# Decoder layer with mixture of experts: three of each token's four expert rows added by DMA, the fourth by VectorE

## The chip, the cores and the metric

The kernel runs on one core of one Trainium2 chip. The metric is the device time of one execution, in microseconds (us); lower is better. A core has TensorE (matrix products), VectorE, ScalarE, GpSimd and SyncE, which run their own instruction streams and meet at semaphores. DMA transfers are issued by SyncE (its queue is "q1 hardware_dynamic" in the profile) and by GpSimd ("q0 software_dynamic"), and both run on the core's 16 DMA engines.

## What is computed

One decoder layer over 512 tokens of width 1024, in float32: an attention and time-mixing half, whose output is added to `x`, and then a feed-forward half in which each token goes to 4 of 32 experts. Only the end of it matters here:

```
h   = rmsnorm(x, ffn_norm_w)
top 4 of 32 experts for each token, gates = softmax(top values)
y_k = gate_k * (act(h @ mlp1_w[e_k] + mlp1_b[e_k]) @ mlp2_w[e_k] + mlp2_b[e_k])
x   = x + y_0 + y_1 + y_2 + y_3
out = rmsnorm(x, final_norm_w)          # x * rsqrt(mean(x*x) + eps) * w
```

## The kernel before

**Tiles.** The 512 tokens are four groups t = 0..3 of 128, one token to a partition; `x` is an on-chip tile of 128 x 4 x 1024. The experts are visited one after the other (b = 0..31), each for the up to 128 tokens that chose it, and the bodies for b = 2..31 are a loop on every engine. The outer rounds exist for experts chosen by more than 128 tokens; with these inputs only round 0 runs.

**The weight stream.** An expert's weights come in 12 pieces of 1 MB. SyncE loads each piece into one of six slots of `raw` (w_pieces, line 1438) after VectorE is done with the piece six before it (`s_lo`). ScalarE splits off the high part (`hi`, line 1547), VectorE the rest (`lo`, line 1672), both in rings of four slots, and TensorE multiplies (lines 1860, 1863, 1881, 1886).

**Expert rows.** ScalarE scales an expert's output by the gate into `ys`, and GpSimd scatters it (line 1499) into `y_dram` in HBM (expert_rows in the profile), which has four rows for each token, one for each k. GpSimd waits until each scatter has landed before it goes on. The table was filled with zeros earlier, so a row that nobody wrote adds nothing. The view `rows_v[t, :, k, :]` is the k-th row of all tokens of group t: 128 rows of 4 KB, with a pitch of 16 KB in HBM.

**The last two experts** (b = 30 and 31) are not scattered. Their outputs stay on chip as high and low parts (`y_hi`, `y_lo`), and TensorE multiplies them with transposed choice matrices (`choose`, line 1971) and with the gated biases (`down_bias`, line 1966) into PSUM, a pair of banks for each group. VectorE makes the two low parts in `y_rest(0, 4)` and `y_rest(1, 0)` (line 1782); ScalarE makes the high parts (lines 1631, 1635). `s_hot` counts the groups that are complete in PSUM.

**The adding transfers.** After its loop GpSimd waits for the last turned rows (`s_tx`), loads the final norm weight, spread over 128 partitions, into `fw` (which is `xg`, the buffer of gathered rows, line 1513), and then issues 16 transfers of 512 KB that add `rows_v[t, :, k, :]` onto `x[:, t, :]` (line 1519), in the order k = 0..3 and, within k, t = 0, 3, 1, 2 (`LAST_ROWS`). Additions onto the same group must not overlap, so for k > 0 it waits until the previous one of that group has landed (`s_row[t]`).

**The close.** For n, t over `LAST_ROWS`, VectorE waits for `s_hot` and for the four additions of group t and sums PSUM and `x` (line 1801). ScalarE squares and sums the row (line 1639) and takes the root (line 1641); `finish(n)` on VectorE takes the reciprocal (line 1792) and multiplies x by it and by `fw` (line 1796); SyncE stores the result (line 1455). `finish(n - 1)` stands behind the sum of group n in VectorE's order, and `finish(3)` is last.

Of the kernel before, what the change touches and what calls it, by code (L numbers as in the profile page):

```python
# [23 lines left out]
ALU = mybir.AluOpType  # L24
# [3 lines left out]
P = 128  # L28
D = 1024
S = 512  # L30
NT = S // P
# [10 lines left out]
EXPERTS = 32  # L42
TURNS = EXPERTS + 1
INDEXED = EXPERTS + 2
SCATTERED = EXPERTS - 2
LAST_ROWS = (0, 3, 1, 2)
# [1306 lines left out]
def place(b, p):  # L1353

    if isinstance(b, int) and b == 0:
        return p - DOWN
    if isinstance(b, int) and b == EXPERTS + 1:
        return STREAM - DOWN + p
    return b * PIECES + (p - 2 * DOWN)


def raw_slot(b, p):

    return place(b if isinstance(b, int) else 1, p) % RAW
# [9 lines left out]
def experts(nc, d, sb, sem, st, g, route, con, ident, psum, bank, out):  # L1374
# [3 lines left out]
    x, stat, o_t, y_dram, down_b, turned = (g[k] for k in ("x", "stat", "o_t", "y_dram", "down_b", "turned"))  # L1378
# [22 lines left out]
    s_tx, s_xh, s_xl = sem("rows_turned"), sem("x_hi"), sem("x_lo")  # L1401
    s_u, s_x, s_sig, s_act = sem("up_clipped"), sem("gate_times_up"), sem("gate_sigmoid"), sem("act_ready")
    s_ta, s_ah, s_al, s_y, s_scat = sem("act_turned"), sem("act_hi"), sem("act_lo"), sem("y_ready"), sem("rows_scattered")
    s_round, s_stored, s_part = sem("round_moved"), sem("rows_stored"), sem("dma_about_to_start")
    s_st, s_selt, s_yl, s_hot = sem("choice_turned"), sem("choice_copied"), sem("last_y_lo"), sem("last_rows_chosen")
    s_blank = sem("gates_blanked")
    s_row = [sem(f"rows_added{t}") for t in range(NT)]
    s_fw, s_add, s_ss, s_sd, s_rs, s_o, s_out = (sem(n) for n in ("final_w_loaded", "sums_ready", "x3_squared", "x3_deviation", "x3_rstd",
                                                                  "out_ready", "out_stored"))
    s_sel31, s_wiped = sem("last_selected"), sem("expert_rows_wiped")  # L1410
# [3 lines left out]
    fw, final = xg, (uu, sg, av, ys)  # L1414
    gate_last = [tab[:, e, 2:3] for e in (EXPERTS - 2, EXPERTS - 1)]
    rows_v = y_dram.rearrange("(t p k) n -> t p k n", p=P, k=4)
    last_banks = {0: 2, 3: 6, 1: 4, 2: 0}

    pairs = psum[:, 0:4, :].rearrange("p b (n two) -> p (b n) two", two=2)
    block = st.enter_context(nc.Block())  # L1420

    def rounds(eng, run, again=None):
        run(0)
        with eng.Fori(1, ROUNDS) as r:
            flag = eng.value_load(flags[0:1, bass.ds(r, 1)])
            with eng.If(flag == 1):
                if again:
                    again(r)
                run(r)

    @block.sync
    def _(sp):
        def load(r, b, p):

            slot = raw_slot(b, p)
            sp.wait_ge(s_lo, r * STREAM + (place(b, p) + 1))
            src = down_rows(d, b - 2, p) if p < DOWN else gate_up_rows(d, b, p - DOWN)
            sp.dma_start(raw[:, slot].rearrange("p r n -> p (r n)"), src).then_inc(s_raw[slot], 16)

        def rest(r):  # L1440

            for p in range(DOWN + RAW, PIECES):
                load(r, 0, p)
            for p in range(DOWN, PIECES):
                load(r, 1, p)
            with sp.Fori(2, EXPERTS) as b:
                for p in range(PIECES):
                    load(r, b, p)
            for b in (EXPERTS, EXPERTS + 1):
                for p in range(DOWN):  # L1450
                    load(r, b, p)

            for n, t in enumerate(LAST_ROWS):
                sp.wait_ge(s_o, r * NT + (n + 1))
                sp.dma_start(out[0, t * P:(t + 1) * P, :], final[t][:]).then_inc(s_out, 16)

        route["sync"](sp)
        rest(0)
        with sp.Fori(1, ROUNDS) as r:
            flag = sp.value_load(flags[0:1, bass.ds(r, 1)])  # L1460
            with sp.If(flag == 1):
                for p in range(DOWN, DOWN + RAW):
                    load(r, 0, p)
                rest(r)
                sp.wait_ge(s_out, (r * NT + NT) * 16)
                sp.sem_inc(s_part, 1)
        sp.wait_ge(s_out, NT * 16)

    @block.gpsimd
    def _(pool):  # L1470
        def zero_rows():
            nc.gpsimd.memset(xg[:], 0.0).then_inc(s_z, 1)

        g["zero_rows"] = zero_rows
        route["gpsimd"](pool)
        pool.wait_ge(s_z, 1)
        pool.sem_inc(s_stored, 1)
        pool.sem_inc(s_blank, 1)

        def gather(r, m):  # L1480
            pool.wait_ge(s_tab, r * INDEXED + (m + 1))
            pool.wait_ge(s_tx, (r * TURNS + m) * 2 + 1)
            pool.sem_inc(s_part, 1)
            nc.gpsimd.tensor_copy(gath_i[:], tab[:, bass.ds(m, 1), 0:1].rearrange("p a c -> p (a c)")).then_inc(s_gi, 1)  # L1484
            pool.wait_ge(s_gi, r * TURNS + (m + 1))
            pool.sem_inc(s_part, 1)
            nc.gpsimd.indirect_dma_start(xg[:], None, g["h2_dram"], bass.IndirectOffsetOnAxis(gath_i[:, 0:1], 0),  # L1487
                                         bounds_check=S - 1, oob_is_err=False).then_inc(s_gath, 16)

        def prepare(r, e):  # L1490
            pool.sem_inc(s_part, 1)
            nc.gpsimd.tensor_copy(this_i[:], tab[:, bass.ds(e, 1), 1:2].rearrange("p a c -> p (a c)"))
            nc.gpsimd.tensor_copy(this_g[:], tab[:, bass.ds(e, 1), 2:3].rearrange("p a c -> p (a c)")).then_inc(s_this, 1)

        def scatter(r, e):
            pool.wait_ge(s_this, r * SCATTERED + (e + 1))
            pool.wait_ge(s_y, r * EXPERTS + (e + 2))
            pool.sem_inc(s_part, 1)
            nc.gpsimd.indirect_dma_start(g["y_dram"], bass.IndirectOffsetOnAxis(this_i[:, 0:1], 0), ys[:], None,  # L1499
                                         bounds_check=4 * S - 1, oob_is_err=False).then_inc(s_scat, 16)  # L1500
            pool.wait_ge(s_scat, (r * SCATTERED + e) * 16 + 16)
            pool.sem_inc(s_stored, 1)

        def run(r):
            for m in range(3):
                gather(r, m)
            with pool.Fori(2, EXPERTS) as b:
                prepare(r, b - 2)
                gather(r, b + 1)
                scatter(r, b - 2)  # L1510
            pool.wait_ge(s_tx, (r * TURNS + EXPERTS) * 2 + 3)
            pool.sem_inc(s_part, 1)
            nc.gpsimd.dma_start(fw[:], d["final_norm_w"].to_broadcast([P, D])).then_inc(s_fw, 16)
            for k in range(4):
                for t in LAST_ROWS:
                    if k:
                        pool.wait_ge(s_row[t], (r * 4 + k) * 16)
                        pool.sem_inc(s_part, 1)
                    nc.gpsimd.dma_start(x[:, t, :], rows_v[t, :, k, :], accum_op=ALU.add).then_inc(s_row[t], 16)

        def again(r):
            pool.wait_ge(s_o, r * NT)
            pool.sem_inc(s_part, 1)
            nc.gpsimd.memset(turned[:].bitcast(F32), 0.0).then_inc(s_blank, 1)
            nc.gpsimd.memset(xg[:], 0.0).then_inc(s_z, 1)
            pool.wait_ge(s_z, r + 1)
            pool.sem_inc(s_part, 1)
            for n in range(4):
                nc.gpsimd.dma_start(y_dram[n * S:(n + 1) * S, :].rearrange("(a p) n -> p a n", p=P),
                                    xg[:].rearrange("p (a n) -> p a n", a=1).to_broadcast([P, S // P, D])).then_inc(s_wiped, 16)  # L1530
            pool.wait_ge(s_wiped, r * 64)
            pool.sem_inc(s_part, 1)

        rounds(pool, run, again)

    @block.scalar
# [113 lines left out]
    def _(dve):  # L1650
# [73 lines left out]
        def run(r):  # L1724
# [55 lines left out]
            def y_rest(n, first):  # L1780
                dve.wait_ge(s_y, r * EXPERTS + (EXPERTS + n))
                nc.vector.scalar_tensor_tensor(y_lo[n], psum[:, first:first + 2, :].rearrange("p b n -> p (b n)"), gate_last[n],
                                               y_hi[n].bitcast(F32), ALU.mult, ALU.subtract).then_inc(s_yl, 1)

            dve.wait_ge(s_used, r * STREAM + (place(b + 1, 0) + 1 + RING))
            y_rest(0, 4)
            y_rest(1, 0)

            def finish(n):
                t = LAST_ROWS[n]  # L1790
# [6 lines left out]

            for n, t in enumerate(LAST_ROWS):
                dve.wait_ge(s_hot, r * NT + (n + 1))
                dve.wait_ge(s_row[t], r * 64 + 64)  # L1800
                nc.vector.tensor_tensor(x[:, t, :], psum[:, last_banks[t]:last_banks[t] + 2, :].rearrange("p b n -> p (b n)"), x[:, t, :],  # L1801
                                        ALU.add).then_inc(s_add, 1)
                if n:
                    finish(n - 1)
            finish(NT - 1)
# [228 lines left out]
```

## Time and profile before

| | |
|---|---|
| three runs | 1722.74, 1724.41, 1724.60 us; median 1724.41 |
| the profiled execution's own time | 1721.57 us |
| its span in the trace | 1719.7 us |
| mean granted TensorE clock | 0.965 of full speed |
| TensorE matmuls busy | 1586.7 us, 92% of the span |
| VectorE, ScalarE, GpSimd busy | 1409.6, 1051.1, 316.3 us |
| HBM read, written | 454.97 MB, 28.31 MB |

The trace is one execution. Its times are counted from the start of the span, so 1719.7 is the end. Busy shares over the whole span are an average over stages with different limits, and what bounds the last 60 us has to be read there. In the DMA view a line of a queue gives packets, megabytes and the time that its packets took as a share of 16 engines over the window; packets overlap a little, so that share can pass 100%. Time to landing runs from the issue of a transfer to its semaphore.

### The profile page before, as it was taken

To read this page: it belongs to the slowest core of one execution; us is meant where nothing else is said; L and a number is where in the kernel's file an instruction comes from. 1 tells how busy PE (TensorE), PEld (TensorE's weight loads), DVE (VectorE), ACT (ScalarE), POOL (GpSimd) and SP (SyncE) were. 2 spreads that over 40 slices of the span, in tenths; PEclk is the share of its full clock that TensorE was granted. 3 is DMA by queue.
4 is the path that set the end of the run, shared out by engine and by line. 5 is a ranking of instruction groups with operands and counts; after the bars stand their busy time and mean duration, and the time that the engine had idled before them with its cause. 6 is when DMAs were issued, how large, how long until landed. Compare 5 with 4: busy or idle time off the path is not lost.

```text
span 1719.7 us, 27994 instructions
## 1 busy us (share of the span) xinstructions
PE 1586.7 (92%) x10297; PEld 1278.6 (74%) x10298; DVE 1409.6 (82%) x1288; ACT 1051.1 (61%) x970; POOL 316.3 (18%) x223
## 2 busy tenths in 40 slices
PE   5888889887687999999999999999999999999994
PEld 5666667666575888888888888888888888888883
DVE  5857667475647899999999999999999999999984
ACT  5434232232335777777777777777777777777772
POOL 6200000000011112222221222112222121311222
PEclk9999999998788999999999999999999999999997
DMA  5610011000629799999999999999999999999999
GB/s 189 245 36 27 26 38 39 26 2 2 212 103 377 280 367 364 368 351 370 360 375 371 351 374 370 366 377 342 366 364 366 357 358 367 359 363 376 353 326 208
DMA packets 100717, 467.39 MB, mean 272 GB/s; under 512 B 12695, under 2 KB 39351, under 8 KB 51376
## 3 DMA queue, kind: packets, MB, share of 16 engines
q1 hardware_dynamic: 86032, 429.79, 65.7%
q0 software_dynamic: 14624, 36.74, 6.9%
q8 instruction: 45, 0.74, 0.2%
q14 instruction: 16, 0.13, 0.0%
HBM read 454.97 MB, written 28.31 MB: 281 GB/s over the span
## 4 chain that ended last, share of the span: by engine, by line
PE 68%; DMA 3%; DVE 2%; ACT 1%; issue 0%; PEld 0%; POOL 0%; ACTq 0%; DVEq 0%; POOLq 0%; PEldq 0%
PE psum L1860 28%; PE psum L1863 13%; PE psum L1881 13%; PE psum L1886 6%; PE psum L1289 3%; DMA x<-expert_rows 2%; PE psum L1852 2%; PE psum L1842 2%; PE psum L1872 1%; PE psum L1832 1%; DVE w_pieces_lo L1672 1%; ACT w_pieces_hi L1547 0%; PE psum L1305 0%; PE psum L1297 0%; DVE x L1801 0%
## 5 line engine op out<-in xcount | busy, mean ns | idle before, releaser
L1672 DVE TENSOR_TENSOR w_pieces_lo<-w_pieces,w_pieces_hi 128x2048 fp32r<-128x2048 f32 x384 | 871.2, 2290 | 92.6 <-ACT w_pieces_hi L1547 92.6
L1547 ACT ACTIVATE w_pieces_hi<-w_pieces 128x2048 fp32r<-128x2048 f32 x384 | 736.8, 1919 | 295.5 <-PE psum L1863 219.1
L1860 PE MATMUL psum<-w_pieces_hi,xh 128*128 128x512 f32 x1024 | 292.5, 408 | 6.1 <-DVE xl L1683 6.1
L1863 PE MATMUL psum<-w_pieces_lo,xh 128*128 128x512 f32 x1024 | 276.5, 392 | 0.0
L1860 PE MATMUL psum<-w_pieces_hi,xl 128*128 128x512 f32 x1024 | 276.4, 392 | 0.0
L1860 PEld LDWEIGHTS psum<-w_pieces_hi,xl 128*128 128x128 f32 x1024 | 192.9, 188 | 43.0
L1863 PEld LDWEIGHTS psum<-w_pieces_lo,xh 128*128 128x128 f32 x1024 | 192.9, 188 | 42.8
L1860 PEld LDWEIGHTS psum<-w_pieces_hi,xh 128*128 128x128 f32 x1024 | 181.7, 190 | 47.8 <-issue 10.9
L1499 POOL DMA_INDIRECT expert_rows<-ys,this_i x30 | 151.9, 5063 | 247.9 <-issue 247.9
L1881 PE MATMUL psum<-w_pieces_hi,ah 128*128 128x512 f32 x512 | 160.9, 395 | 0.0
L1881 PE MATMUL psum<-w_pieces_hi,al 128*128 128x512 f32 x512 | 158.3, 390 | 0.0
L1886 PE MATMUL psum<-w_pieces_lo,ah 128*128 128x512 f32 x512 | 137.0, 390 | 0.0
L1881 PEld LDWEIGHTS psum<-w_pieces_hi,al 128*128 128x128 f32 x512 | 96.2, 188 | 20.2
L1886 PEld LDWEIGHTS psum<-w_pieces_lo,ah 128*128 128x128 f32 x512 | 96.1, 188 | 20.1
L359 ACT ACTIVATE pall<-psum 128x512 f32<-128x512 f32 x26 | 15.5, 594 | 152.9 <-PE psum L781 152.9
L1881 PEld LDWEIGHTS psum<-w_pieces_hi,ah 128*128 128x128 f32 x512 | 93.7, 188 | 18.1 <-DVE al L1689 0.5
L781 PE MATMUL psum<-h_hi_sb,w_hi_sb 128*128 128x512 f32 x208 | 92.6, 445 | 8.8 <-ACT pall L359 8.8
L1487 POOL DMA_INDIRECT xg<-h_rows,gath_i x33 | 81.4, 2468 | 28.7 <-POOL gath_i L1484 27.4
L781 PE MATMUL psum<-h_hi_sb,w_lo_sb 128*128 128x512 f32 x208 | 84.8, 407 | 0.0
L781 PE MATMUL psum<-h_lo_sb,w_hi_sb 128*128 128x512 f32 x208 | 84.7, 407 | 0.0
L1484 POOL CAST gath_i<-index_table 128x1 int32 (+1 forms) x33 | 9.0, 273 | 371.9 <-PE psum L1842 360.6
L1118 POOL DMA_DIRECT2D w_pieces<-in_ffn_norm_w x1 | 0.5, 547 | 383.9 <-POOLq L159 383.9
(366 smaller groups left out, 1973.7 us busy)
## 6 DMA issues: line engine op xcount, KB each, us to landing
w_pieces<-in_mlp_w SPq DMA_DIRECT2D x384, 1024.0 KB, 6.9
w_raw<-in_w_in SPq DMA_DIRECT2D x26, 512.0 KB, 3.9
expert_rows<-o_t POOLq DMA_DIRECT2D x4, 2048.0 KB, 14.7
x<-expert_rows POOLq DMA_DIRECT2D x16, 512.0 KB, 9.5
w_pieces<-in_w_out SPq DMA_DIRECT2D x8, 512.0 KB, 9.2
chunk_work<-in_x SPq DMA_DIRECT2D x4, 512.0 KB, 5.8
x<-in_x SPq DMA_DIRECT2D x4, 512.0 KB, 14.2
h_rows<-w_pieces POOLq DMA_DIRECT2D x4, 512.0 KB, 2.9
```

The costliest lines, as they stand in the source:

```text
L781: last = nc.tensor.matmul(o, w[:, n % 3, k, :], h[:, k, :], start=k == 0 and m == 0, stop=k == KT - 1 and m == 2)
L1289: last = nc.tensor.matmul(bank(2 * t + c), o[:, k, t * P:(t + 1) * P], w[:, k, c * 512:(c + 1) * 512], start=k == 0 and m == 0, stop=k == ...
L1487: nc.gpsimd.indirect_dma_start(xg[:], None, g["h2_dram"], bass.IndirectOffsetOnAxis(gath_i[:, 0:1], 0), bounds_check=S - 1, oob_is_err=Fal ...
L1499: nc.gpsimd.indirect_dma_start(g["y_dram"], bass.IndirectOffsetOnAxis(this_i[:, 0:1], 0), ys[:], None, bounds_check=4 * S - 1, oob_is_err= ...
L1547: nc.scalar.activation(hi[:, p % RING], raw[:, raw_slot(b, p)].rearrange("p r n -> p (r n)"), ACT.Copy).then_inc(s_hi, 1)
L1672: nc.vector.tensor_tensor(lo[:, p % RING], raw[:, raw_slot(b, p)].rearrange("p r n -> p (r n)"), hi[:, p % RING].bitcast(F32), ALU.subtrac ...
L1842: last = nc.tensor.transpose(bank(into, k * P, k * P + P), xg[:, (4 * q + k) * P:(4 * q + k + 1) * P], ident)
L1852: last = nc.tensor.transpose(bank(into, k * P, k * P + P), rows[:, k // 2, k % 2, :], ident)
L1860: nc.tensor.matmul(bank(c), a[:, k, :], hi[:, p % RING, c * 512:(c + 1) * 512], start=False, stop=False)
L1863: last = nc.tensor.matmul(bank(c), xh[:, k, :], lo[:, p % RING, c * 512:(c + 1) * 512], start=False, stop=k == KT - 1)
L1881: nc.tensor.matmul(bank(into + c), a[:, 2 * p + r2, :], hi[:, p % RING, r2 * D + c * 512:r2 * D + (c + 1) * 512], start=p == 0 and r2 == 0 ...
L1886: last = nc.tensor.matmul(bank(into + c), ah[:, 2 * p + r2, :], lo[:, p % RING, r2 * D + c * 512:r2 * D + (c + 1) * 512], start=False, sto ...
```

## The change

For each group t, the rows k = 0, 1, 2 are still added to `x` by DMA, now from the end of GpSimd's loop on, ahead of the wait for the last turned rows and of the norm weight's load, which stand behind the sixth addition. The order of the twelve is written out: (t0,0) (t1,0) (t2,0) (t3,0) (t0,1) (t1,1), the norm weight, (t0,2) (t1,2) (t2,1) (t3,1) (t2,2) (t3,2), where t0..t3 are the groups 0, 3, 1, 2. The row k = 3 is loaded by SyncE, by a plain transfer, into two rows of `o_t`, an on-chip tile that is free by then, after SyncE's last weight load and after all scatters have landed. VectorE adds it to `x` in `add_row(n)`, which waits for the three additions of its group and for the plain load, and counts `s_sum`. `add_row(0)` and `add_row(1)` stand behind `y_rest(0, 4)` and `y_rest(1, 0)`; `add_row(2)` and `add_row(3)` stand behind the sums of the first and the second group.

```diff
+    def row3(t):
+        return o_t[:, 2 * t:2 * t + 2, :].rearrange("p a s -> p (a s)")
@@ SyncE, behind its last weight load
+            sp.wait_ge(s_scat, (r * SCATTERED + SCATTERED) * 16)
+            for t in LAST_ROWS:
+                sp.dma_start(row3(t), rows_v[t, :, 3, :]).then_inc(s_row3[t], 16)
@@ GpSimd, behind its loop over the experts
-            pool.wait_ge(s_tx, (r * TURNS + EXPERTS) * 2 + 3)
-            pool.sem_inc(s_part, 1)
-            nc.gpsimd.dma_start(fw[:], d["final_norm_w"].to_broadcast([P, D])).then_inc(s_fw, 16)
-            for k in range(4):
-                for t in LAST_ROWS:
-                    if k:
-                        pool.wait_ge(s_row[t], (r * 4 + k) * 16)
-                        pool.sem_inc(s_part, 1)
-                    nc.gpsimd.dma_start(x[:, t, :], rows_v[t, :, k, :], accum_op=ALU.add).then_inc(s_row[t], 16)
+            t0, t1, t2, t3 = LAST_ROWS
+            for t, k in ((t0, 0), (t1, 0), (t2, 0), (t3, 0), (t0, 1), (t1, 1), (t0, 2), (t1, 2), (t2, 1), (t3, 1), (t2, 2), (t3, 2)):
+                if k:
+                    pool.wait_ge(s_row[t], (r * 3 + k) * 16)
+                    pool.sem_inc(s_part, 1)
+                nc.gpsimd.dma_start(x[:, t, :], rows_v[t, :, k, :], accum_op=ALU.add).then_inc(s_row[t], 16)
+                if t == t1 and k == 1:
+                    pool.wait_ge(s_tx, (r * TURNS + EXPERTS) * 2 + 3)
+                    pool.sem_inc(s_part, 1)
+                    nc.gpsimd.dma_start(fw[:], d["final_norm_w"].to_broadcast([P, D])).then_inc(s_fw, 16)
@@ VectorE, its close
+            def add_row(n):
+                t = LAST_ROWS[n]
+                dve.wait_ge(s_row[t], r * 48 + 48)
+                dve.wait_ge(s_row3[t], r * 16 + 16)
+                nc.vector.tensor_tensor(x[:, t, :], x[:, t, :], row3(t), ALU.add).then_inc(s_sum, 1)
+
             y_rest(0, 4)
+            add_row(0)
             y_rest(1, 0)
+            add_row(1)
...
             for n, t in enumerate(LAST_ROWS):
                 dve.wait_ge(s_hot, r * NT + (n + 1))
-                dve.wait_ge(s_row[t], r * 64 + 64)
+                dve.wait_ge(s_sum, r * NT + (n + 1))
                 nc.vector.tensor_tensor(x[:, t, :], psum[:, last_banks[t]:last_banks[t] + 2, :].rearrange("p b n -> p (b n)"), x[:, t, :],
                                         ALU.add).then_inc(s_add, 1)
+                if n < 2:
+                    add_row(n + 2)
                 if n:
                     finish(n - 1)
             finish(NT - 1)
```

## Rows read from the trace of the kernel before

**Rows 1.** The page: shares of the chain that ended last, by engine.
```profile
PE 68%; DMA 3%; DVE 2%; ACT 1%; issue 0%; PEld 0%; POOL 0%; ACTq 0%; DVEq 0%; POOLq 0%; PEldq 0%
```

**Rows 2.** That chain in order of time: start us, us, what; the end.
```profile
1663.05 0.58 POOL xg L1513
...
1664.21 10.94 DMA x<-expert_rows
...
1695.99 0.51 issue
1696.50 9.39 DMA x<-expert_rows
1705.98 1.23 DVE x L1801
```

**Rows 3.** Timeline of GpSimd: start us, us, instruction [idle before it, releaser].
```profile
1642.24 5.06 POOL L1499 DMA_INDIRECT expert_rows<-ys,this_i  x1 [8.26 <-issue]
1663.05 0.58 POOL L1513 DMA_DIRECT2D xg<-in_final_norm_w  x1 [15.74 <-PEq L1947]
1663.62 3.61 POOL L1519 DMA_DIRECT2D x<-expert_rows  x4
1673.06 0.85 POOL L1519 DMA_DIRECT2D x<-expert_rows  x1 [5.83 <-DMA x<-expert_rows]
...
1701.48 0.86 POOL L1519 DMA_DIRECT2D x<-expert_rows  x1 [1.48 <-DMA x<-expert_rows]
```

**Rows 4.** DMA view, 1670 to 1706: queue, packets, MB, share.
```profile
q0 software_dynamic: 2063, 7.53, 105.8%
```

**Rows 5.** Timeline of TensorE: the first al, and the last matmuls.
```profile
1692.32 1.52 PE L1971 MATMUL psum<-al,xh 128*128 128x512 f32 x6
...
1695.49 0.61 PE L1971 MATMUL psum<-al,xh 128*128 128x512 f32 x2
```

**Rows 6.** Timelines of VectorE, then SyncE: the close.
```profile
1703.51 1.23 DVE L1801 TENSOR_TENSOR x<-psum,x 128x1024 f32<-128x1024 f32 x1 [13.99 <-DMA x<-expert_rows]
1705.98 1.23 DVE L1801 TENSOR_TENSOR x<-psum,x 128x1024 f32<-128x1024 f32 x1 [1.25 <-DMA x<-expert_rows]
...
1708.58 1.22 DVE L1801 TENSOR_TENSOR x<-psum,x 128x1024 f32<-128x1024 f32 x1
...
1714.07 1.28 DVE L1796 SCALAR_TENSOR_TENSOR av<-x,stat,xg 128x1024 f32<-128x1024 f32 x1
...
1715.38 0.33 SPq L1455 DMA_DIRECT2D out<-av  x1
```

**Rows 7.** DMA view, 4 to 6, plain loads: packets, MB, share.
```profile
q1 hardware_dynamic: 203, 0.77, 95.4%
```

**Rows 8.** The last five scatters (line 1499, 1500 to 1720).
```profile
DMA to landing us min/median/max: 12.4/12.6/13.0
```

**Rows 9.** DMA view, 1666 to 1668.
```profile
q0 software_dynamic: 52, 0.21, 62.6%
q1 hardware_dynamic: 43, 0.24, 29.9%
```

**Rows 10.** DMA view, 1658 to 1666.
```profile
DMA packets 384, 2.82 MB, mean 352 GB/s; under 512 B 40, under 2 KB 40, under 8 KB 40
...
q1 hardware_dynamic: 384, 2.82, 100.4%
```

**Rows 11.** DMA view, 1644 to 1648.
```profile
q1 hardware_dynamic: 216, 1.64, 99.2%
```

**Rows 12.** Timelines of SyncE and ScalarE: last load, last split.
```profile
1661.42 0.33 SPq L1438 DMA_DIRECT2D w_pieces<-in_mlp_w  x1
...
1676.70 1.92 ACT L1547 ACTIVATE w_pieces_hi<-w_pieces 128x2048 fp32r<-128x2048 f32 x1
```

**Rows 13.** DMA view, 1652 to 1654, a scatter beside weights.
```profile
q1 hardware_dynamic: 95, 0.66, 80.8%
q0 software_dynamic: 84, 0.12, 16.4%
```

**Rows 14.** Timeline of VectorE: the second y_rest.
```profile
1688.23 1.28 DVE L1782 SCALAR_TENSOR_TENSOR al<-psum,index_table,ah 128x1024 fp32r<-128x1024 f32 x1 [3.44 <-ACT ah L1635]
```

**Rows 15.** Plain 512 KB stores from GpSimd (line 1130).
```profile
DMA to landing us min/median/max: 2.9/2.9/3.0
```

**Rows 16.** DMA view, 1710 to 1712.
```profile
q0 software_dynamic: 6, 0.01, 3.3%
```

More of the change, by code:

```diff
@@ L1407, in experts @@
     s_row = [sem(f"rows_added{t}") for t in range(NT)]
+    s_row3 = [sem(f"last_row_loaded{t}") for t in range(NT)]
+    s_sum = sem("rows_summed")
     s_fw, s_add, s_ss, s_sd, s_rs, s_o, s_out = (sem(n) for n in ("final_w_loaded", "sums_ready", "x3_squared", "x3_deviation", "x3_rstd",
```

## The prediction

> **What bounds the kernel now.** I read the page first, then the chain of waits over the last 80 us, then the timelines of GpSimd, VectorE, ScalarE, TensorE and SyncE there, and last the DMA view cut into short windows.
>
> Over the whole span TensorE holds 68% of the chain [rows 1]. The change touches none of that; it touches the last 60 us. There the chain runs through one thing: from 1663.05 to 1705.98 it is the expert rows being added to x by DMA, then VectorE's closing work [rows 2]. GpSimd shows the order: the last scatter is issued at 1642.24, the norm weight's load at 1663.05, four additions behind it, then one addition each time an earlier one of the same token group has landed; the last is issued at 1701.48 [rows 3]. Meanwhile the software queue moves 7.53 MB in the 36 us from 1670 with its engines' time full (105.8%) [rows 4]. One addition is 512 KB = 0.524 MB, so 0.524 / (7.53 / 36) = 2.5 us each; 16 cost 40 us. So this stretch is bound by DMA throughput, not latency, and what counts is how much DMA work stands ahead of the closing work. TensorE's last matmuls begin at 1695.49 [rows 5]: it has some 10 us to spare.
>
> How the end hangs on landings: VectorE's second sum (t=3) starts at 1705.98 when the 14th addition lands, and from there sums and final multiplies run back to back until the last output store, 1719.7 - 1705.98 = 13.7 us in all [rows 2, 6]. Additions 15 and 16 land behind that VectorE work at nearly its pace.
>
> **The change part by part.**
>
> *Which landing sets the end.* VectorE's order becomes: sum t=0, row-add t=1; sum t=3, row-add t=2, then finish(0), sum, finish(1), sum, finish(2), finish(3). The row-add of the last group waits for that group's third addition, which is the last transfer of all (T), and everything that followed the second sum before now follows this row-add. A row-add is a 128x1024 tensor-tensor add; the nearest row is the sum from PSUM, 1.22 us [rows 6]. It takes the place of the second sum, of the same length. So end = T + 13.7, where before it was (14th landing) + 13.7: two extra row-adds are early and idle-covered, but finish(0) no longer overlaps the last landings. The row-add for t=1 and sum t=3 (2.5 us) fit just between the last two landings, 2.5 us apart.
>
> *DMA work ahead of T.* Before, 14 additions and the norm weight; after, 12 additions, the norm weight and four plain row loads. The weight's load cancels wherever it stands. Two additions fewer: -5.0 us. Four plain loads: a plain load of 4 KB rows through SyncE's queue moved 0.77 MB in 2 us at 95.4% [rows 7], hence 1.3 us per 0.524 MB, or +5.2 us. This is the cheap bound; the dear one is an addition's 2.5 us (+10.0). I take 1.3: same kind of queue, packet and direction.
>
> *Earlier start.* The last scatter lands 12.6 us after issue [rows 8], at 1654.8; 0.5 us from landing to next issue [rows 2] gives 1655.3 for the first addition instead of 1663.6. The first data lags: the norm weight issued at 1663.05 has no packet in its queue before 1666, and then 62.6% of the 2 us up to 1668 [rows 9], so 3.4 us. Additions thus flow from 1658.7 instead of 1666.5. But the engines are not free then: expert weights move 2.82 MB in 1658 to 1666, 352 GB/s at a share of 100.4% [rows 10], against 1.64 MB in 4 us, 410 GB/s, when the queue is full [rows 11]. Spare is 14% of 7.8 us = 1.1 us, because SyncE's loads are gated by freed slots. Bounds: 0 (the share says full) and, were the traffics independent, all of it (rival below). I take 1.1. Of the 8.3 us gained in issue, only this is worth anything; the rest delays weights.
>
> *The delayed weights.* Sharing halves, the remaining 2.8 MB (6.9 us alone) lasts until 1658.7 + 13.8 = 1672.5, where the last load, issued at 1661.42, had its split at 1676.70 [rows 12]. So nothing is late. At a third of the share it would end at 1679.4, and TensorE would be 2.7 us late, still inside its 10 us. That the two queues do share follows from the scatter, whose 84 packets went beside 95 of weights in 2 us [rows 13].
>
> *Waits on GpSimd and SyncE.* The wait for the turned rows (met at 1663.05) now stands behind the sixth addition; that is issued only after two landings, later than 1663, so it holds up nothing. The row loads stand behind SyncE's last weight load and the scatter wait, met at 1654.8; behind them are only the stores. They take 12.1 us of engine time together with the weights, all spent before 1658.7 + 24.2 = 1683.
>
> *The new wait on VectorE.* Row-add t=0 stands between the two y_rest steps, and waits for the seventh addition. The norm weight with latencies cost 1673.06 - 1666.5 - 2.5 - 0.6 (weights) = 3.5 us [rows 3, 9]; 1658.7 + 7 x 2.5 + 3.5 + 12.1 = 1691.8. The second y_rest, at 1688.23 before [rows 14], then starts at 1693.0 and ends at 1694.3, while TensorE wanted it at 1692.32 [rows 5]. TensorE ends 2 us later, near 1698. VectorE needs the first choice only by 1701, so this is covered; the cover is some 6 us.
>
> *Fewer transfers in flight.* The last two additions wait for those just ahead, with only one other in flight. If landing to next data takes over 2.5 us, engines idle. Beside weights it takes 0.5 + 3.4 = 3.9, a 1.4 us hole; in a quiet queue a 512 KB store landed 2.9 us after issue, data included [rows 15], leaving 1.6 + 0.5 = 2.1 and no hole. Weights are gone by then: I take 0, bounds 0 to 1.4. The Trainium skill, DMA: Bandwidth & Descriptors, Anatomy of one DMA, gives about 2.0 us fixed for a transfer from GpSimd plus bytes over 436 GB/s: by that, an estimate, no hole either, but 1.2 us per row load, so a sum 0.4 us lower than by the row, whose measured rate I use.
>
> **Sum.** T = 1705.98 - 5.0 + 5.2 - 1.1 = 1705.1; end 1718.8 against 1719.7: 0.9 us less. The profiled execution took 1721.57 for its span of 1719.7, so 1720.7; the median is 2.8 above that execution, so 1724.41 - 0.9 = 1723.5. The forecast is no change: a 0.2% step, 3.4 us, is about what a measurement of this kernel can tell from none. Its own bounds: no spare (+1.1), the hole (+1.4), and the last landings: after 1710 the queue moves only 0.01 MB [rows 16], so additions 15 and 16 took 4.2 us from 1705.98, not 5.0. If the last landings come 0.8 us closer together, T is 0.8 earlier, or VectorE, still at its two instructions, eats that again. With all of it, 1722.7 to 1726.0.
>
> **Rivals.** *Additions overlap weights for free (faster).* If additions are limited by their own queue, T = 1658.7 + 12 x 2.5 + 3.5 = 1692.2, and TensorE's end (first choice at 1693.3) leads: three VectorE adds of 1.22 and 13.7 us give 1710.7, a median of 1715.4. For: share read 105.8% at half the bytes. Against: 211 GB/s is half of 410, as if an addition carried its bytes twice through full engines, and nothing of the first addition landed before 1673. Partial overlap gives part of it. Chance 0.15.
>
> *Row loads cost as much as additions (slower).* Each at 2.5: +4.8, so 1728.3. For: short rows at a 16 KB pitch, never loaded so here. Against: [rows 7]. It decides above 2.4 us a load. Chance 0.10.
>
> *Mixing wastes engine time (slower).* In 1666 to 1668, 0.24 MB of weights (0.6 us at 410 GB/s) and 0.21 MB of the software queue (1.0 us at 209) fill 1.6 of 2 us [rows 9]: 20% lost. Over 24.2 mixed us that is 4.8 us, so 1728.3; it passes 0.2% from 18%. Against: that window holds the queue's start. Chance 0.11.
>
> *The change does not do what it says.* The VectorE add replaces a DMA addition, yet the row still travels; if the software queue gets little share while weights run, the early start gains nothing: 1724.6, inside the forecast.
>
> **Chances.** Forecast 0.64, rivals 0.15, 0.10, 0.11. Faster by over 0.2%: 0.16; within: 0.63; slower: 0.21. The range 1720.0 to 1728.6 leaves out most of the free overlap and a little above.
>
> **What the profile would show.** First addition issued near 1655.3; software queue busy beside weights from 1659; row loads landed by about 1684; row-add t=0 near 1692 with y_rest behind it; the last addition landing near 1705; VectorE back to back for 13.7 us from there. A last landing before 1702 would speak for overlap; after 1708, for dear loads or mixing losses, told apart by the megabytes in mixed windows. TensorE's last choice after 1703 would make the new VectorE wait the cause.

## The result, and the profile after

The changed kernel is slower: 1726.57 us median of 20 runs against 1724.40 of 20 runs before, ratio 1.0015 with a 95% interval of 1.0008 to 1.0022, so +2.6 us (0.0015 x 1724.4; the interval reaches from +1.4 to +3.8 us). The forecast was -0.9 us. The size of the step is within the 0.2% that I called no change, but its sign is the other one and clear of the noise.

GpSimd's timeline of the kernel after answers to [rows 3]:

```profile
1643.24 5.07 POOL L1508 DMA_INDIRECT expert_rows<-ys,this_i  x1 [8.26 <-issue]
1656.63 3.68 POOL L1525 DMA_DIRECT2D x<-expert_rows  x4 [8.33 <-DMA expert_rows<-ys,this_i]
1668.44 0.86 POOL L1525 DMA_DIRECT2D x<-expert_rows  x1 [8.13 <-DMA x<-expert_rows]
1673.40 0.86 POOL L1525 DMA_DIRECT2D x<-expert_rows  x1 [4.10 <-DMA x<-expert_rows]
1673.97 0.85 POOL L1529 DMA_DIRECT2D xg<-in_final_norm_w  x1
1685.18 0.85 POOL L1525 DMA_DIRECT2D x<-expert_rows  x1 [10.35 <-DMA x<-expert_rows]
1688.95 2.61 POOL L1525 DMA_DIRECT2D x<-expert_rows  x3 [2.93 <-DMA x<-expert_rows]
1698.71 0.85 POOL L1525 DMA_DIRECT2D x<-expert_rows  x1 [7.15 <-DMA x<-expert_rows]
1701.19 0.85 POOL L1525 DMA_DIRECT2D x<-expert_rows  x1 [1.62 <-DMA x<-expert_rows]
```

The last scatter is issued 1.0 us later than in the trace of before, a difference of these two executions that lies ahead of anything the change touches. To be free of it I count from that issue below. The additions do start 7 us earlier. But look at the end: from 1689 GpSimd issues three at once, then nothing for 7.15 us, then the last two. The order is behind the first gap too. GpSimd issues strictly in the written order, and (t0,2) and (t1,2), which wait for landings at 1684.6 and 1688.4, stand ahead of (t2,1) and (t3,1), whose predecessors had landed at 1677.0 and 1680.8 (semaphore times of this trace). VectorE's timeline answers to [rows 6, 14]:

```profile
1692.44 1.22 DVE L1800 TENSOR_TENSOR x<-x,o_t 128x1024 f32<-128x1024 f32 x1 [6.66 <-DMA x<-expert_rows]
1693.59 1.28 DVE L1792 SCALAR_TENSOR_TENSOR al<-psum,index_table,ah 128x1024 fp32r<-128x1024 f32 x1
...
1705.26 1.23 DVE L1800 TENSOR_TENSOR x<-x,o_t 128x1024 f32<-128x1024 f32 x1 [7.18 <-DMA x<-expert_rows]
1706.40 1.22 DVE L1819 TENSOR_TENSOR x<-psum,x 128x1024 f32<-128x1024 f32 x1
1709.22 1.23 DVE L1800 TENSOR_TENSOR x<-x,o_t 128x1024 f32<-128x1024 f32 x1 [1.59 <-DMA x<-expert_rows]
...
1717.30 1.28 DVE L1814 SCALAR_TENSOR_TENSOR av<-x,stat,xg 128x1024 f32<-128x1024 f32 x1
```

The last landing is at 1709.2, that is 66.0 us after the last scatter's issue, where I had 1705.1 - 1642.2 = 62.9. From there to the end at 1722.9 it is 13.7 us, as forecast. The whole error is in the landing. The DMA view shows where; lines are queue, packets, MB, share, for 1674 to 1684, 1690 to 1698, 1698 to 1702 and 1704 to 1708 in this order:

```profile
q0 software_dynamic: 376, 1.35, 67.5%
q1 hardware_dynamic: 377, 1.41, 37.2%
...
q0 software_dynamic: 417, 1.51, 103.1%
...
q0 software_dynamic: 136, 0.49, 79.2%
...
q0 software_dynamic: 124, 0.44, 58.7%
```

While both queues have work the engines are full (67.5 + 37.2%). Once the additions are alone, they move 1.51 MB in 8 us where [rows 4] gives 1.67, then 0.49 MB in 4 us where it gives 0.84, and 0.44 in 4 near the end. Before, that rate held from 1670 to 1706. In the first of these stretches the engines' time is still full (103.1%) and its packets are longer: 41 of its 369 additions' packets of 4 KB took over 340 ns, where 328 is the rule; in the kernel before it was 11 of 1838 (1670 to 1706). From 1698 on the engines also stand idle (79.2 and 58.7%, the last with the end of the transfers in it). These are holes.

### The profile page after: what moved, and what is told of

Its sections match the earlier page's. It is cut to its first block, busy times and chain, and to the rows that moved or that the text cites. A ratio compares the mean times of both kernels' runs of the same rounds, so it can differ in the third digit from the quotient of the medians.

```text
span 1722.9 us, 27998 instructions
## 1 busy us (share of the span) xinstructions
PE 1585.8 (92%) x10297; PEld 1277.5 (74%) x10298; DVE 1412.4 (82%) x1292; ACT 1051.4 (61%) x970; POOL 313.0 (18%) x219
## 4 chain that ended last, share of the span: by engine, by line
PE 67%; DMA 4%; DVE 2%; issue 1%; ACT 1%; POOL 0%; POOLq 0%; ACTq 0%; DVEq 0%
PE psum L1880 27%; PE psum L1883 13%; PE psum L1901 13%; PE psum L1906 6%; DMA x<-expert_rows 3%; PE psum L1289 3%; PE psum L1872 2%; PE psum L1862 2%; PE psum L1892 1%; DMA expert_rows<-ys,this_i 1%; PE psum L1852 1%; DVE w_pieces_lo L1682 1%; ACT w_pieces_hi L1557 0%; DMA w_pieces<-in_w_out 0%; PE psum L1305 0%
```

## The experiments

Ratios are to the kernel before, timed beside each, with 95% intervals. Four series were timed at different times: the changed kernel; e1 to e4; e6 to e9; changed_again and e10 to e12. changed_again is the changed kernel once more. "Landing" is the last one that VectorE's closing chain waits for; it and "end" are in us, counted from the issue of the last scatter, and come from one trace of each kernel.

| kernel | ratio [95%] | landing | end |
|---|---|---|---|
| before | 1 | 63.7 (14th) | 77.5 |
| changed | 1.0015 [1.0008, 1.0022] | 66.0 | 79.7 |
| changed_again | 1.0013 [1.0004, 1.0022] | 65.1 | 78.9 |
| e1_order | 0.9994 [0.9985, 1.0003] | 62.2 | 75.9 |
| e2_early_only | 0.9996 [0.9987, 1.0005] | 63.1 (14th) | 76.8 |
| e3_rows_only | 1.0008 [0.9998, 1.0018] | 63.3 | 77.1 |
| e4_close | 1.0001 [0.9992, 1.0010] | 68.1 | 78.1 |
| e6_yrest_first | 1.0023 [1.0014, 1.0033] | 65.7 | 79.5 |
| e7_no_row_loads | 0.9996 [0.9987, 1.0006] | 60.4 | 74.1 |
| e8_lone_last | 1.0034 [1.0024, 1.0044] | 69.2 | 83.0 |
| e9_presum | 0.9966 [0.9954, 0.9979] | 62.5 | 71.3 |
| e10_three | 0.9988 [0.9979, 0.9997] | 62.4 | 76.1 |
| e11_presum_uneven | 0.9982 [0.9973, 0.9991] | 67.0 | 75.8 |
| e12_presum_late | 0.9981 [0.9972, 0.9990] | 62.3 | 71.1 |

### e1_order: another order of the additions

```diff
-            for t, k in ((t0, 0), (t1, 0), (t2, 0), (t3, 0), (t0, 1), (t1, 1), (t0, 2), (t1, 2), (t2, 1), (t3, 1), (t2, 2), (t3, 2)):
+            for t, k in ((t0, 0), (t1, 0), (t2, 0), (t3, 0), (t0, 1), (t1, 1), (t2, 1), (t3, 1), (t0, 2), (t1, 2), (t2, 2), (t3, 2)):
```

> The changed kernel with one edit: the twelve additions go row by row (all four groups' k = 0, then k = 1, then k = 2), so that each waits for one issued four places earlier; the norm weight stays behind the sixth. Theory 'holes' (the last additions each had one other transfer in flight, and the time from a landing to the next data let the DMA engines run dry): the last landing comes 3 us earlier than in the changed kernel (1709.2), near 1706, and the kernel is 2 to 3.5 us faster than the changed one, so about equal to the kernel before (-1 to +0.5 us). Rival 'shared engines' (row loads or mixing cost more than the sum): same megabytes, no change, +2.6 us over before. Rival 'VectorE's new wait': row-add t=0 now waits for the ninth addition, some 5 us later, y_rest and TensorE's choices move as far, and the kernel gets slower still, +4 us or more over before.

Measured 0.9994, 0.21% or 3.6 us under the changed kernel's ratio (another series), and -1.0 us against before. The landing moves from 66.0 to 62.2. GpSimd's timeline of e1_order:

```profile
1689.03 0.85 POOL L1525 DMA_DIRECT2D x<-expert_rows  x1 [2.91 <-DMA x<-expert_rows]
1692.90 0.85 POOL L1525 DMA_DIRECT2D x<-expert_rows  x1 [3.02 <-DMA x<-expert_rows]
1695.59 0.85 POOL L1525 DMA_DIRECT2D x<-expert_rows  x1 [1.84 <-DMA x<-expert_rows]
```

and its DMA view, 1690 to 1702:

```profile
q0 software_dynamic: 691, 2.51, 105.8%
```

That is the rate of [rows 4] (209 GB/s) again, without a hole, and only 3 of 613 packets of 4 KB took over 340 ns. "Holes" holds, "shared engines" falls. "VectorE's new wait" falls as a cause of the loss too, though half of it came true: y_rest did move 5 us later and TensorE waited 7 us (its line stands in the last section), and the kernel still got faster.

### e10_three and e8_lone_last: how deep the queue must be

```diff
 e8_lone_last
+                if (t, k) == (t3, 2):
+                    pool.wait_ge(s_row[t2], (r * 3 + 3) * 16)
+                    ...
 e10_three: the order from the seventh on
+            (t0, 2), (t2, 1), (t3, 1), (t1, 2), (t2, 2), (t3, 2)
```

> The changed kernel with the very last addition waiting for the landing of the one before it as well, so that it is alone in the engines and its time from issue to landing can be read. 'Holes': far above its 2.5 us of engine time, by the latency beside weights 3.4 + 2.5 = 5.9 us or more, and the kernel is slower than the changed one by what the two had overlapped, 2 to 3 us. If the latency in a quiet queue is that of the store (1.6 us): 4.1 us from issue to landing, and the change of time under 1 us.

Measured 1.0034, some 3.3 us over the changed kernel (another series). The lone addition in GpSimd's timeline and the DMA view of 1708 to 1710, e8_lone_last:

```profile
1700.67 0.85 POOL L1528 DMA_DIRECT2D x<-expert_rows  x1 [7.20 <-DMA x<-expert_rows]
1707.87 0.85 POOL L1528 DMA_DIRECT2D x<-expert_rows  x1 [6.35 <-DMA x<-expert_rows]
```

```profile
q0 software_dynamic: 17, 0.07, 37.5%
```

The row-add behind it starts here:

```profile
1714.46 1.22 DVE L1803 TENSOR_TENSOR x<-x,o_t 128x1024 f32<-128x1024 f32 x1 [4.76 <-DMA x<-expert_rows]
```

So it takes 1714.44 - 1707.87 = 6.6 us from issue to landing, with empty engines. The packet records of the same trace (times in us from the span's start) split it:

```
landing of the addition before                 1707.32
issue of the lone addition                     1707.87
first data packet                              1709.41
first 28 packets (before 1710.5)               median 605 ns, up to 1300 ns
other packets                                  median 328 ns; each of the 16 engines has eight in all
end of an engine's data, median of 16          1712.79
the 16 engines report: first, median, last     1712.7, 1713.1, 1714.4
```

From landing to issue it is 0.5 us, to the first data 1.5, for eight packets 3.4 where 8 x 328 ns make 2.6, to the report of the median engine 0.3, and from there to the slowest engine, which alone makes the landing, 1.3. Landing to landing a dependent addition takes 7.1 us. The store from which I had read the latency [rows 15] needs 2.9 in all. It gave the time to the first data rightly (2.1 us from landing to first data, as in my sum), but nothing of what comes behind.

> The changed kernel with its additions ordered so that from the seventh on each one waits for the addition three places earlier, and two others are in flight behind it (t0's third addition still seventh). From e8_lone_last a dependent addition takes 0.5 + 6.5 = 7.0 us from landing to landing. 'Holes' by that number: two in flight give one addition each 3.5 us, three give 7.0 / 3 = 2.3, under the 2.5 of the engines. So three are as good as four: the last landing within 1 us of e1_order's, 3 to 4 us before the changed kernel's, and -2.5 to -3.6 us against the changed kernel. Rival: the loss comes from having fewer than four (the queue must be deep): half of that gain or less.

Measured 0.9988, 0.25% or 4.3 us under the changed kernel in the same series (1.0013), and its landing is e1_order's (62.4 and 62.2). Three in flight are as good as four, as 7.1 / 3 = 2.4 is under 2.5. Two give 7.1 / 2 = 3.5 us for each by this sum; in the traces the last two landings behind (t3,1) took 8.5 us (changed), 7.2 (changed_again) and 8.2 (e6_yrest_first), so 3.6 to 4.3 us each.

### e2_early_only and e3_rows_only: the parts by themselves

The edits are shortened here; `load fw` stands for the norm weight's load with its semaphore.

```diff
 e2_early_only (edit of the kernel before)
-            pool.wait_ge(s_tx, ...); load fw
             for k in range(4):
                 for t in LAST_ROWS:
                     ...
+                    if t == t1 and k == 1:
+                        pool.wait_ge(s_tx, ...); load fw
 e3_rows_only (edit of the changed kernel)
+            pool.wait_ge(s_tx, ...); load fw
+            for k in range(3):
+                for t in LAST_ROWS:
```

> The kernel before with the early start alone: all sixteen additions by DMA, row by row, from the end of GpSimd's loop on, the norm weight behind the sixth; VectorE as before. 'Work-conserving engines': worth only the spare of 1658 to 1666, -1 us against before (1723.4). Rival 'additions overlap the weights for free': -8 us or more. Rival 'mixing wastes engine time': 0 to +2 us. 'Holes' expects none here, since four stay in flight.

> The changed kernel with its start put back: the wait for the turned rows and the norm weight's load first, then the twelve additions row by row; the fourth rows still loaded by SyncE and added by VectorE. If a plain row load costs 1.3 us of the engines: two additions fewer ahead of the closing work (-5.0) and four loads more (+5.2), +0 to +1 us over before. If it costs an addition's 2.5 us: +5 us. 'Holes' expects none (four in flight).

The early start alone gives 0.9996, -0.7 us, and the landing is 0.6 us earlier (63.1 against 63.7); the interval reaches from -2.2 to +0.9 us. Free overlap (-8 us) is out. The row loads alone give 1.0008, +1.4 us with an interval from -0.3 to +3.1; an addition's price (+5 us) is out. Neither part by itself shows a loss that is clear of noise, though e3_rows_only's interval does not exclude 2.6 us. What shows that the loss comes with the order is e1_order and e10_three, which have both parts and another order.

### e7_no_row_loads: the price of the row loads

```diff
-            sp.wait_ge(s_scat, (r * SCATTERED + SCATTERED) * 16)
-            for t in LAST_ROWS:
-                sp.dma_start(row3(t), rows_v[t, :, 3, :]).then_inc(s_row3[t], 16)
...
-                dve.wait_ge(s_row3[t], r * 16 + 16)
-                nc.vector.tensor_tensor(x[:, t, :], x[:, t, :], row3(t), ALU.add).then_inc(s_sum, 1)
+                nc.vector.tensor_tensor(x[:, t, :], x[:, t, :], av[:], ALU.add).then_inc(s_sum, 1)
```

> The changed kernel without the four plain row loads and their waits; it leaves out the fourth row, and VectorE's row-add reads another tile of the same shape. A price measurement: if a row load costs 1.3 to 1.4 us of the engines, which are full until 1688 in the changed kernel, all later landings come 5.2 to 5.5 us earlier and the kernel is 5.2 to 5.5 us faster than the changed one (-2.8 us against before). If they cost an addition's 2.5 us: -10 us against the changed one. If they ran in gaps of the additions: 0.

The kernel leaves out the fourth rows. VectorE's last row-add in its trace:

```profile
1703.72 1.22 DVE L1796 TENSOR_TENSOR x<-x,av 128x1024 f32<-128x1024 f32 x1 [1.04 <-DMA x<-expert_rows]
```

The landing is at 60.4, against 66.0 in the changed kernel and 65.1 in changed_again: 4.7 to 5.6 us for four loads, by which of the two traces is taken. The packet records of the changed kernel say the same from below: in 1674 to 1684 a 4 KB row load packet takes 173 ns (median of 341) beside additions, 8 of them on each engine, 1.4 us a load. The timed difference is smaller, 0.19% or 3.3 us (0.9996 against 1.0015, from different series, and each interval reaches 1.2 to 1.7 us to either side), so it is compatible with 5 us only near its edge. Both exclude an addition's 2.5 us a load (10 us in all) and free loads.

### e6_yrest_first: the new wait on VectorE

```diff
             y_rest(0, 4)
-            add_row(0)
             y_rest(1, 0)
+            add_row(0)
             add_row(1)
```

> The changed kernel with the second y_rest ahead of row-add t=0, so that TensorE no longer waits for an addition. 'Holes' (the last landing sets the end): y_rest starts at 1689 instead of 1693.6, TensorE ends 1.4 us earlier, the last landing stays near 1709 and the time is that of the changed kernel, +2.6 us over before. Rival 'VectorE's new wait': the loss goes away, 0 against before.

Measured 1.0023, no faster than the changed kernel (another series). TensorE's timeline, the changed kernel and then e6_yrest_first:

```profile
1694.92 1.65 PE L1991 MATMUL psum<-al,xh 128*128 128x512 f32 x6 [1.44 <-DVE al L1792]
```

```profile
1694.02 1.52 PE L1991 MATMUL psum<-al,xh 128*128 128x512 f32 x6
```

The 1.44 us wait is there and goes away, and nothing hangs on it (landing 65.7, end 79.5): the wait was covered.

### e4_close: another order of the close

```diff
-            for n, t in enumerate(LAST_ROWS):
...
+            total(0); total(1); finish(0); finish(1)
+            add_row(2); total(2); add_row(3); total(3); finish(2); finish(3)
```

In the kernel each of these stands on its own line; `total(n)` is the sum from PSUM with its waits.

> The changed kernel with VectorE's close in another order: sums of the first two groups and their finish first, then row-add, sum of the third group, row-add, sum of the fourth, and the last two finishes. The last landing stays at 1709.2. If the close after it is what my sum says (row-add, two sums and three finishes in 13.7 us), it shrinks to one row-add, one sum, ScalarE's square and root, one finish and the store, 9.8 us: -3.9 us against the changed kernel, -1.3 us against before. If the closing work were bound elsewhere (ScalarE, the stores), no change.

Measured 1.0001, -2.4 us against the changed kernel, not -3.9. The close is 10.0 us (78.1 - 68.1; expected 9.8), but the landing is 2.1 us later. SyncE's timeline of e4_close, and the DMA view of 1702 to 1712:

```profile
1702.55 0.34 SPq L1464 DMA_DIRECT2D out<-uu  x1
1703.94 0.34 SPq L1464 DMA_DIRECT2D out<-ys  x1
```

```profile
q1 hardware_dynamic: 288, 1.05, 26.7%
```

Two stores of 512 KB now run on the same engines as the last addition, issued at 1702.64. Their packets take 26.7% of 10 us, 2.7 us of all engines, which is enough for the 2.1. That they are the cause is the likely reading; no run takes them away.

### e9_presum, e11_presum_uneven, e12_presum_late: a version faster than both

With the even order, e1_order is bound by VectorE, which is never idle for more than 0.2 us from the row-add at 1697.5 to the last finish. One sum can be had earlier: PSUM is added onto the loaded row before the additions land. The edit against the changed kernel, shortened (it also has e1_order's order of additions, and its `add_row` is gone):

```diff
+            def from_psum(n):                       # row3 += PSUM, needs only TensorE and the load
+                dve.wait_ge(s_hot, r * NT + (n + 1))
+                dve.wait_ge(s_row3[t], r * 16 + 16)
+                nc.vector.tensor_tensor(row3(t), psum[...], row3(t), ALU.add).then_inc(s_sum, 1)
             y_rest(0, 4)
-            add_row(0)
             y_rest(1, 0)
-            add_row(1)
...
+            for n in range(NT):
+                from_psum(n)
             for n, t in enumerate(LAST_ROWS):
                 dve.wait_ge(s_sum, r * NT + (n + 1))
+                dve.wait_ge(s_row[t], r * 48 + 48)
+                nc.vector.tensor_tensor(x[:, t, :], x[:, t, :], row3(t), ALU.add).then_inc(s_add, 1)
                 if n:
                     finish(n - 1)
```

> A version that the runs so far point to: the additions row by row as in e1_order, the second y_rest not behind any addition, and VectorE adds the PSUM sum onto the loaded fourth row as soon as TensorE has it, so that only one add (x plus that sum) is left behind each landing. Landings as in e1_order (1697.5, 1700.0, 1702.5, 1705.0); behind each, one add and one finish, 2.5 us; end = last landing + 8.7 = 1713.7, less a store that now runs beside the last addition (1.3 us): -3.5 to -5 us against before. Rival: if VectorE's close were bound by something else than its order, as e1_order, -1 us.

Measured 0.9966 [0.9954, 0.9979], 1716.58 us median of six runs beside 1722.92 of before: -5.9 us by the ratio, a little more than expected. VectorE's timeline of e9_presum:

```profile
1693.51 4.62 DVE L1800 TENSOR_TENSOR o_t<-psum,o_t 128x1024 f32<-128x1024 f32 x4 [3.46 <-PE psum L1989]
1698.05 1.22 DVE L1820 TENSOR_TENSOR x<-x,o_t 128x1024 f32<-128x1024 f32 x1
...
1705.47 1.22 DVE L1820 TENSOR_TENSOR x<-x,o_t 128x1024 f32<-128x1024 f32 x1
...
1708.42 1.28 DVE L1813 SCALAR_TENSOR_TENSOR av<-x,stat,xg 128x1024 f32<-128x1024 f32 x1
```

The four PSUM sums fill VectorE's idle time up to the first landing (they end at 1698.1, it comes at 1697.8), and 71.3 - 62.5 = 8.8 us follow the last.

It is e9_presum with the changed kernel's order of additions.

> e9_presum with the changed kernel's order of additions. 'Holes' and the close add up: the last landing stays where the changed kernel has it (1709.2), and 8.7 us of close follow it instead of 13.7: -4 to -5 us against the changed kernel, 3 to 4 us slower than e9_presum, -2 us against before. Rival: with the shorter close the order no longer matters, and it equals e9_presum.

0.9982, 0.31% under the changed kernel in its series (-5.3 us), and some 2.8 us over e9_presum (another series, so between 0 and 5.5). By the traces the order still costs: the end is 4.5 us behind e9_presum's. Its landing is even later than the changed kernel's (67.0), with the first store issued at 1704.75 beside the last addition, as in e4_close.

It is e9_presum with the late start: the wait for the turned rows and the norm weight come first.

> e9_presum with the start put back: wait for the turned rows, norm weight, then twelve additions row by row. It prices the early start where the last landing alone sets the end. By the spare of 1.1 us and e3_rows_only's last landing against e1_order's (1 us later, counted from the last scatter): +1 us over e9_presum, -5 us against before. Rival 'additions overlap weights for free': +5 us or more over e9_presum.

0.9981 [0.9972, 0.9990]. By the ratios the late start costs 0.15% or 2.6 us, but the intervals of this and of e9_presum, from different series, leave 0 to 5; by the traces (71.1 and 71.3) nothing. An early start worth more than 5 us is out; whether 1.1 us is right is not settled. Nor do the times of e11 and e12, from one series, bear out what their traces say: the ratios are equal (0.9982 and 0.9981), where the ends of the traces are 4.7 us apart. With the shorter close, what the order costs is so not settled in size.

## Why the prediction was wrong

**Right.** The closing chain: landing + 13.7 us, to 0.1 us. The engine price of additions (327 to 328 ns a 4 KB packet beside weights, beside row loads or alone, 2.5 us each) and of row loads (4.7 to 5.6 us for four by e7_no_row_loads, forecast 5.2). No loss by mixing (104.7% busy in 1674 to 1684). Weights delayed without anyone waiting: TensorE's first matmul behind the last weights (`down_bias`) starts at 1687.88 and before at 1686.88, in both 44.6 us behind the issue of the last scatter. The new wait on VectorE: y_rest at 1693.6 (forecast 1693.0) and covered. With four in flight, e1_order's landing is at 62.2 where my sum has 62.9, and it measures -1.0 us against before, where I forecast -0.9: the sum is that of a kernel without holes.

**Roughly right, not settled in size.** The early start as 1.1 us: e2_early_only has 0.6 in the trace and 0.7 in the runs, with 0 inside its interval.

**Wrong: "Fewer transfers in flight ... I take 0, bounds 0 to 1.4".** The step failed in what it compared. It set the time from a landing to the next data, 2.1 us, against the 2.5 us of engine work in the other transfer, and 2.1 was right (e8_lone_last: 1709.41 - 1707.32). But at a landing the other transfer's 2.5 us are no longer ahead of most engines. A landing is the report of the slowest engine, in e8_lone_last 1.3 us behind the median one, and 0.3 us lie between an engine's data and its report; the first packets of the next transfer then take 605 ns instead of 328 and cost 0.8 us more. The measured period of a dependent addition is 7.1 us, 4.5 us over its own data at full pace, and one other addition covers 2.5 of them. So from 1698 on an addition takes 3.5 us or more and not 2.5: the last two landings behind (t3,1) are 8.5 us apart from it (changed_again 7.2) where full engines need 5.0, that is 2.2 to 3.5 us lost, where I had put 0. My upper bound for this step, 1.4 us, was too low as well.

I also counted this one place alone. In 1690 to 1698, too, after the queue had drained to one addition before three were issued together at 1689, the engines moved 191 GB/s instead of 211, in 8 us 0.8 us' worth of data less; by the landing of (t3,1) the kernel is 0.2 us behind e1_order's pace (57.4 against 62.2 - 5.0), changed_again 0.7. Together that is the difference of the landings to e1_order, +2.9 to +3.8 us, with which -0.9 turns into +2.0 to +2.9; measured +2.6. Why an engine's packets are slow after the queue has run low stays open: the slow ones stand where it had, but no run separates that from other causes.

By the Trainium skill, DMA: Bandwidth & Descriptors, Anatomy of one DMA, 2.0 us plus bytes over 436 GB/s give, as an estimate, 3.2 us for 512 KB, where the lone addition took 6.6: its rule does not hold for an adding transfer here.

So the change does two things that about cancel (one row of each group moved from the adding to the plain path, and an early start) and a third that does not show in the megabytes: an order in which the last additions depend on those just issued.

## What to carry to other kernels

Where DMA transfers depend on one another, compare the landing-to-landing time of one (here 7.1 us) with the engine time (2.5 us): their ratio, rounded up, is how many independent ones must be in flight, up to the very last (here three, as e10_three bears out). Take the whole period from landing to landing, not only the part up to the next data, and don't take it from another kind of transfer; issue one alone and read it. Where one engine issues them in a fixed order, don't put one that must wait ahead of one that is ready. And once the landing is as early as it gets, move work of the consumer ahead of it (here the PSUM sum), and look whether results stored early run beside the last transfer.

## What the runs showed of the hardware that I had not expected

An adding transfer holds an engine 328 ns for each 4 KB packet. A plain one takes 173 ns beside additions and 159 in the stores at the end; the additions stay at 327 ns beside row loads. After a pause the first packets of an addition took a median of 605 ns. In e8_lone_last the slowest of 16 engines reported 1.3 us behind the median. And TensorE, after the wait in e1_order, came back at half clock; its first products, and its windows (us, then PE, PEld, DVE, ACT, POOL busy with counts, PEclk, DMA share, GB/s):

```profile
1700.01 2.93 PE L1991 MATMUL psum<-al,xh 128*128 128x512 f32 x6 [6.98 <-DVE al L1792]
```

```profile
1694.00:1700.00 6.00, 0.00 (x0) 0.00 (x0) 2.42 (x2) 0.00 (x0) 0.85 (x1) 0.77 1.07 212
1700.00:1703.00 3.00, 2.99 (x7) 2.41 (x8) 2.91 (x3) 0.48 (x1) 0.00 (x0) 0.50 1.01 203
1703.00:1706.00 3.00, 2.84 (x10) 1.89 (x9) 2.90 (x3) 2.03 (x5) 0.00 (x0) 0.82 0.18 36
```

TensorE ran no matmul from 1693.0 to 1700.0. The granted clock fell in that time and is 0.50 (1.2 of 2.4 GHz) until about 1704. The six products took 2.93 us, where the changed kernel's took 1.65 after its wait of 1.44 us. It cost nothing in e1_order, but it is the price that a longer wait behind an addition would have had.
